# Six places for gathered expert rows instead of eight, and three weight loads fewer, in a hybrid inference step

## The reference: what is computed

```python
def peer(h, w_query, keys1, keys2, exp_u, exp_v):           # h: 128 tokens x 1024
    q = (h @ w_query).reshape(T, PEER_HEADS, 2, D_PHALF)      # 8 heads, 2 x 128
    s1 = einsum('thd,nd->thn', q[:, :, 0], keys1)             # 128 keys each
    s2 = einsum('thd,nd->thn', q[:, :, 1], keys2)
    v1, i1 = top_k(s1, 16); v2, i2 = top_k(s2, 16)
    ...                                                       # best 16 of the 256 sums -> e_idx, gate
    u = exp_u[e_idx]
    act = gelu(einsum('thkd,td->thk', u, h))
    return einsum('thk,thkd->td', gate * act, exp_v[e_idx])
```

## Time and profile before

| | |
|---|---|
| median of 3 runs | 1156.53 us (1155.89 to 1156.76) |
| span of the profiled execution | 1155.1 us |
| bytes moved by DMA | 458.68 MB, 402.68 of them on the queue of the gathers |
| PE busy | 875.5 us (76%) |
| DVE busy | 816.8 us (71%) |
| POOL busy | 553.4 us (48%) |
| ACT busy | 448.7 us (39%) |

### The profile page before, as it was taken

The page is one execution under the profiler, slowest core; times in us unless marked ns, Lnnn a source line. Parts: engine busy times, 40 slices in busy tenths (PEclk is TensorE's granted clock), DMA queues, the critical chain, the costliest instruction groups (busy, mean ns, idle before and its releaser), DMA issues.

```text
span 1155.1 us, 12183 instructions
## 1 busy us (share of the span) xinstructions
PE 875.5 (76%) x3735; PEld 397.5 (34%) x3740; DVE 816.8 (71%) x2123; ACT 448.7 (39%) x1413; POOL 553.4 (48%) x437
## 2 busy tenths in 40 slices
PE   8999988997888857665677768587656667666556
PEld 6748644443333424232233333143222122221111
DVE  2426877876686979996777785757886777767544
ACT  2121444433443424433554663343333333333334
POOL 0002444552554745553564563655474554555443
PEclk9999999999997988897898899888898778877779
DMA  9902999999999999999999999999999999999996
GB/s 378 401 1 78 427 424 426 426 426 429 394 422 428 406 427 426 376 421 423 428 427 424 426 427 427 425 427 425 419 380 426 426 427 426 427 426 427 428 426 274
DMA packets 67079, 458.68 MB, mean 397 GB/s; under 512 B 8387, under 2 KB 10179, under 8 KB 15686
## 3 DMA queue, kind: packets, MB, share of 16 engines
q0 software_dynamic: 55888, 402.68, 83.3%
q1 hardware_dynamic: 10982, 54.97, 11.7%
q10 hardware_dynamic: 144, 0.26, 0.1%
HBM read 453.59 MB, written 3.24 MB: 395 GB/s over the span
## 4 chain that ended last, share of the span: by engine, by line
DMA 41%; PE 26%; DVE 16%; POOL 7%; issue 6%; ACT 3%; SPq 0%; POOLq 0%; DVEq 0%
DMA rows<-in_uv,ids 39%; PE ps L581 25%; DVE rows L1991 8%; POOL rows L520 5%; POOL work L505 1%; ACT work L1212 1%; DMA rows<-in_w_qi 1%; ACT wgt L1212 1%; DMA wt<-in_w_q 1%; DMA rows<-in_uv,last_ids 1%; PE ps L584 1%; DVE top L1581 1%; ACT zact L1212 1%; DVE wt L1585 1%; DVE work L1714 0%
## 5 line engine op out<-in xcount | busy, mean ns | idle before, releaser
L520 POOL DMA_INDIRECT rows<-in_uv,ids x380 | 454.1, 1195 | 471.0 <-PE ps L581 402.7
L581 PE MATMUL ps<-rows,work 128*64 128x512 f32 x1536 | 463.1, 733 | 262.5 <-ACT work L1212 261.8
L1991 DVE CUSTOM_DVE_ANT_0 rows<-rows,wt 128x1024 f32<-128x1024 f32 x256 | 314.0, 1227 | 168.5 <-DMA rows<-in_uv,ids 165.0
L1212 ACT ACTIVATE zact<-zdot 128x1 f32<-128x1 f32 x384 | 77.6, 202 | 555.7 <-DVE zdot L1991 555.2
L581 PEld LDWEIGHTS ps<-rows,work 128*64 128x64 f32 x1536 | 107.1, 155 | 525.2 <-ACT work L1212 366.1
L1991 DVE CUSTOM_DVE_ANT_0 rows<-rows,masks 128x1024 f32<-128x1024 f32 x128 | 157.3, 1231 | 51.4 <-DMA rows<-in_uv,ids 48.5
L581 PE MATMUL ps<-wt 128*128 128x128 f32 (+7 forms) x599 | 155.9, 414 | 0.9 <-DMA wt<-in_w_kv 0.9
L1212 ACT ACTIVATE work<-pair,wgt 128x64 f32<-128x64 f32 x384 | 133.5, 348 | 12.5
L1212 ACT ACTIVATE wgt<-zact,gates 128x1 f32<-128x1 f32 x384 | 113.1, 295 | 12.4
L581 PEld LDWEIGHTS ps<-wt 128*128 128x128 f32 (+2 forms) x604 | 89.2, 192 | 55.1 <-issue 46.9
L581 PEld LDWEIGHTS ps<-work,wt 128*128 128x128 f32 (+1 forms) x664 | 85.1, 203 | 55.7 <-issue 55.7
(11 more groups left out here) (168 smaller groups left out, 679.0 us busy)
## 6 DMA issues: line engine op xcount, KB each, us to landing
wt<-in_w_q SPq DMA_DIRECT2D x8, 2048.0 KB, 12.2
rows<-in_uv,ids POOLq DMA_INDIRECT x380, 12.4
rows<-in_w_out SPq DMA_DIRECT2D x2, 2048.0 KB, 32.2
wt<-in_w_out SPq DMA_DIRECT2D x2, 2048.0 KB, 11.8
wt<-in_ckv SPq DMA_DIRECT2D x16, 256.0 KB, 11.0
x<-in_x SPq DMA_DIRECT2D x5, 512.0 KB, 8.6
rows<-in_w_qi SPq DMA_DIRECT2D x1, 2048.0 KB, 12.9
wt<-in_w_qa SPq DMA_DIRECT2D x1, 2048.0 KB, 11.9
```

The source lines that it names most:

```text
L520: pool.indirect_dma_start(row[s], None, a["uv"], bass.IndirectOffsetOnAxis(ap=ids[:, own(n // KP).start + n % KP:own(n // KP).start + n % ...
L581: return nc.tensor.matmul(out, lhsT, rhs, start=start, stop=stop)
L1212: return nc.scalar.activation(*args, **kw)
L1991: V.tensor_tensor_reduce(row[s][:, 0:D], row[s][:, 0:D], h2r[t][:, n % 2, :], 1.0, 0.0, ALU.mult, ALU.add, zdot[:, s:s + 1]).then_inc(dott ...
```

## The change

The ring has six places instead of eight (`G = 6`); `PLACE` no longer names places 4 and 5 of `rows`. They keep the first half of the output weights to the end, so that half isn't loaded again, and slot 4 of `wt`, where it went, receives query slab 3 once the `qkb` projections are done and keeps it. The slabs are loaded in the order 0, 1, 2, 3, 1, 0, 2 instead of 0, 1, 2, 3, 2, 1, 0, 2, 3; the heads of tiles 1 and 2 are worked in another order to match. The held slab is now the fifth load, is used by other units, and its last copies wait for the store of the retention state. Query 6 moves from clock 48 to 54. The first gathers into places 0 to 3 come two rows earlier in the ring's order, and so do their waits.

```diff
--- before.py
+++ after.py
@@ -36,7 +36,7 @@
 NKV = 2 * P + DH + HI
 HP, KP, NK = 8, 16, 128
 UNITS = TILES * HP
-G = 8
+G = 6
 RING = 2
 EPS = 1e-6
 TAKEN = -3.39e38
@@ -112,7 +112,7 @@
         top8 = sb("top8", [P, 8])
         below, gsum, rgsum, euler = sb("below", [P, KP]), sb("gsum", [P, 1]), sb("rgsum", [P, 1]), sb("euler", [P, 1])
 
-        rows = sb("rows", [P, G, 2 * D])
+        rows = sb("rows", [P, 8, 2 * D])
         wt = sb("wt", [P, 6, KC * 512])
         masks = sb("masks", [P, 2 * D])
         work = sb("work", [P, 4128])
@@ -129,7 +129,7 @@
         def at(region, off, n):
             return region[:, off:off + n]
 
-        PLACE = (4, 5, 6, 7, 0, 1, 2, 3)
+        PLACE = (6, 7, 0, 1, 2, 3)
         row = [rows[:, place, :] for place in PLACE]
 
         dmask_a = at(masks, 0, HB * 2 * P).rearrange("p (h i) -> p h i", h=HB)
@@ -268,15 +268,15 @@
         def w_q(k):
             if k == 0:
                 return slot(at(rowf, SLOT, SLOT))
-            return slot(wt[:, 0 if k < 7 else k - 4, :])
+            return slot(wt[:, Q_SLOT[k], :])
 
         w_qi, w_qa = slot(at(rowf, 0, SLOT)), slot(wt[:, 0, :])
         w_out0 = (slot(at(rowf, 2 * SLOT, SLOT)), slot(at(rowf, 3 * SLOT, SLOT)))
         w_vb, w_qkb, w_gb = slot(wt[:, 3, :]), slot(wt[:, 4, :]), slot(wt[:, 5, :])
-        w_out = (slot(wt[:, 4, :]), slot(wt[:, 5, :]))
-
-        w_in = {n: sem("w_" + n) for n in ("kv", "qi", "qa", "vb", "qkb", "gb", "out0", "out1", "out2", "out3")}
-        q_in = [sem(f"q_in{i}") for i in range(4)]
+        w_out = (w_out0[0], slot(wt[:, 5, :]))
+
+        w_in = {n: sem("w_" + n) for n in ("kv", "qi", "qa", "vb", "qkb", "gb", "out0", "out1", "out3")}
+        q_in = [sem(f"q_in{i}") for i in range(3)]
         x_in = [sem(f"x_in{t}") for t in range(TILES)]
         x_again = [sem(f"x_again{t}") for t in range(TILES)]
         g1_in, ident_in, small_in, keys_in = (sem(n) for n in ("g1_in", "ident_in", "small_in", "keys_in"))
@@ -328,18 +328,20 @@
         ATT2 = 154
         Y_BANK = (6, 6, 0)
 
-        Q_LOADS = (0, 1, 2, 3, 2, 1, 0, 2, 3)
+        Q_LOADS = (0, 1, 2, 3, 1, 0, 2)
+        Q_SLOT = (None, 0, 0, 4, 0, 0, 3)
+        Q_SEM = ((0, 1), (0, 2), (0, 3), (1, 1), (0, 4), (0, 5), (2, 1))
         HELD = len(Q_LOADS)
 
         def q_load(u):
             t, h = divmod(u, HP)
-            return (6, HELD, 7, 8)[h // 2] if t == 2 else (0, 3)[t] + h // 2
-
-
-        AHEAD, HURRIED, FAST = (1, 2, 15, 16), (2, 3, 8, 16), (2, 3, 16, 17, 18)
+            return ((0, 1, 2, 3), (2, 3, 4, 5), (5, 3, HELD, 6))[t][h // 2]
+
+
+        AHEAD, HURRIED, FAST = (1, 2, 15, 16), (2, 3, 6, 8, 16), (2, 3, 16, 17, 18)
 
         def q_at(u):
-            return {2: 8, 3: 10, 4: 20, 8: 88, 16: 224, 17: 230}.get(u, 16 * u - 48)
+            return {2: 8, 3: 10, 4: 20, 6: 54, 8: 88, 16: 224, 17: 230}.get(u, 16 * u - 48)
 
         def take_at(u):
             return q_at(u) + (3 if u == 2 else 5 if u in HURRIED else 11)
@@ -402,12 +404,13 @@
             def load_q(k):
                 if k == 1:
                     sp.wait_ge(qa_ps, 3)
-                elif 0 < k < 7:
-                    sp.wait_ge(q_ps, [u for u in range(UNITS) if q_load(u) < k][-1] + 1)
-                if k == 6:
+                elif k in (2, 4, 5):
+                    before = {2: 1, 4: 2, 5: 4}[k]
+                    sp.wait_ge(q_ps, [u for u in range(UNITS) if q_load(u) == before][-1] + 1)
+                if k == 5:
                     sp.wait_ge(q_held, 5)
-                dst = wt[:, 0 if k < 7 else k - 4, :] if k else at(rowf, SLOT, SLOT)
-                sp.dma_start(dst, a[f"w_q{Q_LOADS[k]}"]).then_inc(q_in[max(0, k - 6)], 16)
+                dst = wt[:, Q_SLOT[k], :] if k else at(rowf, SLOT, SLOT)
+                sp.dma_start(dst, a[f"w_q{Q_LOADS[k]}"]).then_inc(q_in[Q_SEM[k][0]], 16)
 
             load_q(0)
             sp.wait_ge(kv_sb, TILES)
@@ -427,14 +430,13 @@
             sp.wait_ge(pv_ps, 3)
             sp.wait_ge(kv_out, 16 * 9)
             sp.dma_start(x[:, 1, :], a["x"][1]).then_inc(x_again[1], 16)
-            load_q(3)
             sp.wait_ge(vb_sb, 3)
             for b in range(STREAMS // 2):
                 sp.dma_start(cki[:, b, :], a["cki"][2 * b:2 * b + 2].rearrange("e d t -> (e d) t")).then_inc(cki_in[b], 16)
             sp.wait_ge(sp_sb, 2)
             sp.dma_start(o["state_p"], snp).then_inc(sp_out, 16)
             sp.wait_ge(qk_ps, 3)
-            sp.dma_start(wt[:, 4, :], a["w_out0"]).then_inc(w_in["out2"], 16)
+            load_q(3)
             sp.wait_ge(gb_ps, 3)
             sp.dma_start(wt[:, 5, :], a["w_out1"]).then_inc(w_in["out3"], 16)
             sp.wait_ge(summed, OWN + 2)
@@ -450,7 +452,6 @@
 
             load_ckv(0)
             load_ckv(1)
-            load_q(5)
             sp.wait_ge(mt_ps, TILES)
             load_ckv(2)
             load_ckv(3)
@@ -458,14 +459,12 @@
                 sp.wait_ge(pv_ps, ATT[2] + b - 3)
                 load_ckv(b)
                 if b == 4:
-                    load_q(6)
+                    load_q(5)
             sp.wait_ge(pv_ps, ATT[2] + STREAMS)
             sp.dma_start(x[:, 2, :], a["x"][2]).then_inc(x_again[2], 16)
-            load_q(7)
+            load_q(6)
             sp.wait_ge(hready, 2 * TILES)
             sp.dma_start(gfb[0:1, :], a["ln_final_g"].partition_broadcast(1)).then_inc(gf_in, 16)
-            sp.wait_ge(wout, 2 * TILES)
-            load_q(8)
             sp.wait_ge(y_out, 1)
             sp.dma_start(o["y"][0], x[:, 0, :]).then_inc(y_done, 16)
             sp.wait_ge(y_out, 2)
@@ -511,9 +510,9 @@
                 s = n % G
                 if n % KP == 0:
                     pool.wait_ge(picked, n // KP + 1)
+                if n == 2:
+                    pool.wait_ge(qi_ps, 3)
                 if n == 4:
-                    pool.wait_ge(qi_ps, 3)
-                if n == 6:
                     pool.wait_ge(q_ps, 2)
                 if n >= G:
                     pool.wait_ge(acc, (n - G) // 2 + 1)
@@ -799,7 +798,7 @@
                     if k == HELD:
                         pe.wait_ge(q_held, 5)
                     else:
-                        pe.wait_ge(q_in[max(0, k - 6)], 16 * (k + 1 if k < 7 else 1))
+                        pe.wait_ge(q_in[Q_SEM[k][0]], 16 * Q_SEM[k][1])
                 e, c0 = part // 4, part % 4 * 2
                 for c in (c0, c0 + 1):
                     head = held_q(h % 2, c) if q_load(u) == HELD else w_q(q_load(u))[:, c, h % 2 * 256:h % 2 * 256 + 256]
@@ -998,7 +997,7 @@
                     if t == 1 and e == 1:
                         yield from until(64)
                         pe.wait_ge(x1_done, 3)
-                    pe.wait_ge(w_in[f"out{2 + e}"], 16)
+                    pe.wait_ge(w_in["out3" if e else "out0"], 16)
                     for c in range(KC):
                         out_part(t, e, c)
                         if c % per == per - 1 or c == KC - 1:
@@ -1504,13 +1503,14 @@
             def keep_queries():
 
                 yield from until(150)
-                act.wait_ge(q_in[0], 16 * 6)
-                slab = w_q(5)
+                act.wait_ge(q_in[0], 16 * 4)
+                slab = w_q(4)
                 for part in range(4):
                     h, c = divmod(4 * part, KC)
                     if part < 3:
                         copy(held[h][:, c:c + 4, :], slab[:, c:c + 4, h * 256:h * 256 + 256]).then_inc(q_held, 1)
                     else:
+                        act.wait_ge(ss_out, 16)
                         copy(held[2], slab[:, 4:7, 256:512]).then_inc(q_held, 1)
                         copy(held[3], slab[:, 7:8, 256:512]).then_inc(q_held, 1)
                     yield
```

## The result

The changed kernel takes 1243.03 us in the median of 4 runs (1236.19 to 1248.74), the kernel before 1156.64 beside it. The ratio is 1.0739, 95% interval 1.0700 to 1.0778: 86 us slower, and outside the range that was forecast, on its dear side. Lines 520, 581, 505 and 1212 of before are 519, 580, 504 and 1211 now.

What follows compares the result with a forecast made beforehand. Bound by bytes over 427 GB/s, plus the start and the dips. 1156.5 - 14.7 (three loads) + 23.9 (two places less) + 7 (POOL's powers) + 2 (the end) = 1174.7, so 1175 us; range 1148 to 1200.

Steps and rivals of the forecast that it cites:

- Bound by bytes at first: Kernel before: time is bytes over 427 GB/s on the DMA engines, plus the start and the dips.
- The three loads: Three dropped weight loads of 2.10 MB, 4.9 us each where DMA engines are full or nearly so: -14.7 us.
- The moves at no cost: Slab 3 has 10 us in hand, the held slab's copies 25 us; for the start's earlier wait nothing is taken.
- What two places less cost: Ring of six: a pair's second row lands 8.1 us after first issue, loop 12.7 or 14.3 us against 14.7; +23.9 us.
- the walk: Count over 187 pairs of how late each lands when issued after the group three back, on an ideal queue: +23.9 us.
- Rival 3: Much slower: in a shallow queue rows do not follow at 2.43 us, late half no longer covered; 1203 us, chance 0.17.
- POOL's part: POOL's power between a pair's two gathers, in 21 of 24 places, delays the second row: +7 us, bounds 0 to 17.
- The end: The third of the last four gathers waits for a group, last issue 4.5 us later: +2 us, 0 to 4.5.
- The deeper dips: Sign of being right: deeper dips in GB/s at 120 to 150, 330 to 380 and 440 to 520 us.
- GB/s of 410 or more after 850 us: Sign of being right: the DMA rate late in the run stays at 410 GB/s or more.
- Rival 1: Faster: late groups are a backlog of landed rows, only the start and 440 to 520 us cost; 1148 us, chance 0.14.
- Rival 2: No change: the first gather is slow because it is first, a row takes 4.5 us; 1157 us, chance 0.07.

Runs made afterwards that it cites:

- half_add8: Kernel before, ring of eight, PE leaving out the second 512 columns of most expert sums: 1157.07 us, ratio 0.9998.
- ring6nl: Kernel before with six places and the three loads left out, none of the change's moves: 1243.56 us, ratio 1.0734.
- alone6: Changed kernel, POOL issuing a pair of gathers only when the pair before has landed: 2094.76 us in one run.
- ring6: Kernel before with six places and nothing else of the change, all loads kept: 1264.92 us, ratio 1.0919.
- gates6: Changed kernel with POOL's powers moved from behind the first gather of a pair to behind the second: 1245.07 us, ratio 1.0747.
- gates6b: Changed kernel with POOL's power for the five hurried units issued sooner, the others as they are: 1247.62 us, ratio 1.0780.
- half_add: PE leaving out the second 512 columns of most expert sums, in both kernels: 1191.29 us in the ring of six, 1157.07 in the ring of eight.
- warm6: Changed kernel with five useless matmuls behind each group from step 268 to 370: median 1232.85 us, ratio 1.0632 from three of four runs.
- half_add6: Changed kernel, PE leaving out the second 512 columns of most expert sums: 1191.29 us, ratio 1.0280.

## Why the prediction was wrong

The sum was 1156.5 - 14.7 + 23.9 + 7 + 2 = 1175, and 1243 was measured.

**Bound by bytes at first: right.** half_add8 says so with no difference at all.

**The three loads, -14.7: right** where they were priced, -13.7 in the ring of eight. In the ring of six they give some 21. If that is more, then presumably because a load in the queue makes each row behind it later and the loop has nothing to absorb it; no run shows this.

**The moves at no cost: right** as far as can be measured. ring6nl and the changed kernel have the same median to 0.6 us, with some 8 us either way for the noise. Slab 3 is issued at 270.95 us, and PE never waits for a query slab; the list of its waits has none. The state's store is issued at 536.3 and the first held copy stands at 579.0.

**The step that failed** is the one under "What two places less cost": "with two transfers 10.6" and "8.1 (5.7 + 2.43) to the landing of its second row". It is 9.5 us with nothing in the queue (alone6) and 11.45 in the changed kernel's run. With 9.5 the loop is 15.5 us (0.44 + 9.5 + 0.42 + 2.65 + 2.49), above the 14.7 that three pairs allow, where I had 14.3 at worst. With the measured prices the walk finds 55 or so late pairs and not 23. Rival 3 had this in it, the 3.7 us between the first two landings. No other pair shown had met an empty queue, so it was the only evidence for the price at issue, and rival 3 with its 0.17 should have been the forecast. It too was too cheap: its 1203 is about half of the way to 1243.

**And the walk itself**, the larger part, was too cheap even with the right price. With the measured 6.0 and 9.5 us in the place of 5.7 and 8.1 it gives 57 us; the ring alone costs 108 (ring6), where my sum had 32.9 for it (23.9 + 7 + 2). Of these 75 us too few the price explains 33 (57 - 23.9), and at least 42 are left to the walk. It prices every pair at an empty queue. In the changed kernel that queue is there for hardly any: of 153 pairs whose landings can be told, 152 have their first row issued while one to four earlier rows are still on their way, and the last of those lands 5.7 us later in the mean. So 9.5 turns into 11.45. What I should have compared is the whole loop: for three pairs to keep the 5.38 us of before, it had to fall from 21.5 to 16.1 us. On an empty queue it is 15.5, so a queue of 0.6 us was all that it could afford, and in stretches without loads (14.7 available) none. It fell to 17.45, and 17.45 / 3 = 5.82 us for a pair are the measured 5.79.

**POOL's part, +7: not borne out.** gates6 shows nothing that can be measured, with some 6 us either way for the noise. DVE's new waits for the powers, 19.4 us, I had not seen coming: the power of a hurried unit stands behind a gather that now waits one pair longer. They cost nothing measurable either (gates6b). **The end, +2:** not isolated; the third of the last gathers does wait for its group,

```profile
1221.43 0.94 POOL L533 DMA_INDIRECT rows<-in_uv,last_ids  x1 [2.30 <-PE ps L580]
...
1230.92 0.95 POOL L539 DMA_INDIRECT rows<-in_uv,last_ids  x1 [0.31 <-issue]
```

2.3 us, and the last issue stands 12.1 us before the end of the span against 14.9 before, 2.8 closer where I had said some 4.

**The signs I had given:** w_q loads 6, right. The median landing between 7 and 8.5 us: 8.8 among the 305 gathers of the changed kernel whose landings are all recorded, just outside. The deeper dips came, 358 GB/s between 462 and 520 us where it was 398, but not they alone. GB/s of 410 or more after 850 us, wrong: 386; "400 GB/s or less in every late slice (rival 3)" is nearly what came, 344 to 402. Rival 1 has no row for it: the landed backlog did shrink (landing to product 0.70 to 0.42 us), and that was 0.3 us of the 5.4 that the loop had to lose (21.5 to 16.1). Rival 2 is out: on an empty queue no gather of 300 to 2000 us landed sooner than 5.4 us (alone6). The Trainium skill's fit for one such transfer (DMA: Bandwidth & Descriptors, Anatomy of one DMA, SWDGE path), by which 4.4 us is the estimate for this row, isn't borne out here: alone6 has 6.0 us in the mean of 172 rows on an empty queue.

**What stays open.** 9.5 us became 11.45 while earlier rows were still on their way and the 16 partial landings of a row stood further apart (1.8 us against 0.8). How the 1.95 us divide between the two no run tells, nor why the packets take longer in a ring of six (last section).

## What to carry to other kernels

A ring of buffers has two limits, bytes over bandwidth and loop latency over buffers in flight, and the room between them is to be read before places are taken: sum the loop with the latency of an empty queue as a whole unit (here a pair, 9.5 us) takes it, not of one transfer plus a transfer time. If that sum, 15.5 us, exceeds (places left) x (time per row), 14.7, expect the loop to set the time, and the loop to be longer than the sum (17.45 here), since the queue is seldom empty. An edit that shortens the end of the loop and nothing else (half_add) tells in one run which of the limits holds; what work added or moved elsewhere gives (gates6, warm6) did not follow the same slope here.

## What the runs showed that was not expected

The worth of a place is far from even: 94 us for the seventh, 14 for the eighth. The busy share of the DMA engines does not tell their rate: 0.98 at 386 GB/s in the changed kernel against 1.01 at 426 before. From the packets' records, one of 8 KB takes 309 ns in the median in both, and 312 in the mean before and 332 after, since 353 of them take over 1 us after and 42 before. Between 925 and 1100 us the means are 310 and 331 ns: longer packets make up 6% of the lower rate, and idle engines (1.01 to 0.98) only 3%. The mean of the whole run is 312 in the ring of eight, 314 in that of seven, 323 in half_add6, 332 in the changed kernel and 359 in alone6, so it grows as fewer rows wait. Part of what looks like busy time may then be an engine that waits inside a packet; no run tests that.
